# Two chained DiT blocks on one core: when the attention of block 1 waits for its PSUM banks, takes its row minima and runs its exponentials

## What is computed

```
def layer(x, cx, ...):                      # block 1, twice; the second time without context outputs
    hx = rmsnorm(x, norm_w) * (1 + scale) + shift
    px = split_cols(hx @ w_in)              # projections of the 512 latent tokens
    pc = split_cols(hc @ w_in)              # and of the 256 context tokens
    ya, yca = global_gqa(...)               # mixer A: 8 heads, keys = 512 latents + 256 context tokens
    yb, ycb = neighbourhood_attn(...)       # mixer B: 8 heads, per query block 256 context + 256 band keys
    yc_, ycc = window_gqa(...)              # mixer C: 8 heads, +-128 window + 256 context + a sink
    x = x + gate * (concat(ya, yb, yc_) * silu(px[9]) @ w_out)

# mixer A, per block of 128 queries:
    q = rmsnorm(q, qn) ; k = rmsnorm(k, kn)         # then rope
    s = einsum('bqhgd,bkhd->bhgqk', q, k_all)       # 128 x 768 scores per head
    p = softmax_f32(s)
    y = einsum('bhgqk,bkhd->bqhgd', p, v_all)
```

## Time and profile before

| | |
|---|---|
| median of 3 runs | 2501.29 us (2499.45 to 2502.21) |
| the profiled execution's own time | 2503.11 us |
| its span, first to last instruction | 2501.0 us |
| PE busy | 2406.2 us, 96% of the span |
| DVE, ACT, POOL busy | 54%, 38%, 19% |
| chain that ended last, share by engine | PE 81%, DVE 5%, ACT 5%, issue 4%, POOL 2% |
| granted PE clock, mean | 0.992 |

### The profile page before, as it was taken

How to read it: one execution, slowest core, us unless ns; L and a number is a source line. 1 busy time by engine, 2 the same in 40 slices (tenths; PEclk the granted TensorE clock), 3 DMA queues, 4 the chain that set the end, 5 groups by cost and what they waited for, 6 DMA issues and landing times.

```text
span 2501.0 us, 40281 instructions
## 1 busy us (share of the span) xinstructions
PE 2406.2 (96%) x16214; PEld 1969.1 (79%) x16214; DVE 1346.8 (54%) x2733; ACT 948.8 (38%) x1659; POOL 470.0 (19%) x287
## 2 busy tenths in 40 slices
PE   8989999999999899999999999999999999999998
PEld 6767878878877678788887668888888667888887
DVE  5667757665326654677739545333336844533333
ACT  5364263542333633554444334222225323422222
POOL 2101211012342012112474231000003241000001
PEclk9999999999999999999999999999999999999999
DMA  7302412134134044124432112223222112223222
GB/s 312 110 2 93 172 62 98 52 128 161 59 109 152 2 149 146 57 110 161 154 140 85 51 54 90 96 82 117 87 92 96 68 51 76 85 83 111 101 78 74
DMA packets 64650, 250.49 MB, mean 100 GB/s; under 512 B 7889, under 2 KB 10449, under 8 KB 54993
## 3 DMA queue, kind: packets, MB, share of 16 engines
q1 hardware_dynamic: 61216, 236.10, 26.6%
q0 software_dynamic: 2592, 11.54, 1.4%
q10 hardware_dynamic: 656, 0.30, 0.0%
HBM read 243.67 MB, written 4.19 MB: 99 GB/s over the span
## 4 chain that ended last, share of the span: by engine, by line
PE 81%; DVE 5%; ACT 5%; issue 4%; POOL 2%; DVEq 2%; DMA 1%; ACTq 1%; SPq 0%; POOLq 0%
PE ps L2650 38%; PE ps L2461 21%; PE ps L593 5%; PE ps L2627 4%; ACT probs L863 2%; PE ps L692 2%; PE ps L634 2%; DVE row_min L769 1%; PE ps L2440 1%; DVEq L772 1%; PE ps L2343 1%; PE ps L677 1%; POOL split_panels_first L1115 1%; DVE ps L780 1%; PE ps L2482 1%
## 5 line engine op out<-in xcount | busy, mean ns | idle before, releaser
L2650 PE MATMUL ps<-h_split,split_panels 128*128 128x512 f32 x2928 | 685.7, 393 | 1.8 <-ACT projected L1574 0.8
L2650 PEld LDWEIGHTS ps<-h_split,split_panels 128*128 128x128 f32 x2928 | 545.9, 188 | 126.9 <-issue 13.7
L2461 PE MATMUL ps<-h_split_first,split_panels_first 128*128 128x512 f32 (+1 forms) x2772 | 546.5, 354 | 4.1 <-POOL h_split_first L1147 2.0
L2461 PEld LDWEIGHTS ps<-h_split_first,split_panels_first 128*128 128x128 f32 x2772 | 446.1, 190 | 78.6 <-issue 8.7
L1115 POOL TENSOR_TENSOR split_panels_first<-panels_first,split_panels_first 128x1024 fp32r<-128x1024 f32 (+1 forms) x102 | 228.2, 2238 | 740.0 <-ACT split_panels_first L1302 740.0
L1984 DVE TENSOR_TENSOR split_panels<-panels,split_panels 128x1024 fp32r<-128x1024 f32 (+2 forms) x171 | 192.6, 1126 | 297.2 <-ACT split_panels L1310 293.4
L1310 ACT ACTIVATE split_panels<-panels 128x1024 fp32r<-128x1024 f32 (+2 forms) x210 | 204.3, 974 | 344.9 <-PE ps L2650 343.6
L1808 DVE SCALAR_TENSOR_TENSOR ps<-modulation_panels,silu_c,ps 128x256 f32<-128x256 f32 x480 | 225.2, 487 | 30.4 <-issue 2.1
L2650 PE MATMUL ps<-ffn_hidden_split,split_panels 128*128 128x512 f32 x990 | 225.0, 389 | 0.0
L2650 PEld LDWEIGHTS ps<-ffn_hidden_split,split_panels 128*128 128x128 f32 x990 | 185.8, 188 | 38.6
L1126 POOL TENSOR_TENSOR probs_turned<-probs_turned,probs 128x512 f32<-128x512 f32 x30 | 42.2, 1408 | 771.3 <-ACT probs L1517 771.3
(11 more groups left out here) (303 smaller groups left out, 2931.0 us busy)
## 6 DMA issues: line engine op xcount, KB each, us to landing
modulation_panels<-in_ada SPq DMA_DIRECT2D x64, 1024.0 KB, 4.8
panels<-in_w SPq DMA_DIRECT2D x88, 512.0 KB, 3.2
panels_first<-in_in SPq DMA_DIRECT2D x72, 512.0 KB, 5.7
panels<-in_in SPq DMA_DIRECT2D x42, 512.0 KB, 3.2
panels_first<-in_out SPq DMA_DIRECT2D x32, 384.0 KB, 3.0
panels<-in_w SPq DMA_DIRECT2D x32, 384.0 KB, 3.1
panels<-in_w SPq DMA_DIRECT2D x32, 320.0 KB, 2.8
panels<-in_out SPq DMA_DIRECT2D x16, 512.0 KB, 3.2
```

What stands on the lines that cost most here:

```text
L2461: ins = mm(at0, split1[:, s, w, c, :], hs1[:, h, c, lo:e], start=c == 0 and i == 0, stop=c == KC - 1 and i == 2)
L2650: ins = mm(out, split[:, n % SPLIT, a, c - base, :], moving(b, c), start=first and i == 0 and j == 0, stop=last and i == len(chunks) - 1 a ...
```

## The change

It has three parts, all in block 1's attention.

1. `scores_pe` waits at its head only for ACT's copy (the first two banks). Where the unit two before has a second copy, PE waits for DVE's copy just ahead of the first matmul that writes the third bank. Mixer A's keys also become one segment of 768 columns instead of 512 and 256, so that head 1's part in the third bank is one matmul of 512 columns instead of two of 256.
2. In mixer A (units with a `"root"`, the context units among them) one reduction takes both heads' minima, through a view of PSUM with the heads as its middle dimension, and one `scalar_tensor_tensor` multiplies both by the negated roots. `max_ready` rises by two at once.
3. In mixer B (sets of two banks) ACT runs `exponentials_act(u)` ahead of `turned_act(prev)`.

```
                     if mixer == "A":
-                        segs = [(0, 0, SEQ), (SEQ, SEQ, TOK)]
+                        segs = [(0, 0, TOK)]
...
             if u["banks_of"] and u["in_sets"]:
-                for ev in u["banks_of"]["events"][-2:]:
-                    if ev["by"] == "act":
-                        pe.wait_ge(pt_by_act, ev["c"] + 1)
-                    else:
-                        pe.wait_ge(pt_by_dve, ev["c"] + 1)
+                pe.wait_ge(pt_by_act, u["banks_of"]["events"][0]["c"] + 1)
...
             last = {}
+            third = u["banks_of"]["events"][1:] if u["banks_of"] and u["in_sets"] else []
             for e, col, a, z in segments(u):
+                if third and e == 1 and col >= 256:
+
+                    pe.wait_ge(pt_by_dve, third.pop()["c"] + 1)
...
+            if "root" in u:
+
+                s, n = 2 * u["i"] % 4, u["at"][1] - u["at"][0]
+                both_heads = ps[:, u["at"][0]:u["at"][0] + 2 * n].rearrange("p (e n) -> p e n", e=2)[:, :, 0:u["w"][0]]
+                V.tensor_reduce(row_min[:, s:s + 2], both_heads, AX_X, ALU.min)
+                dve.drain()
+                V.scalar_tensor_tensor(out=row_min[:, s:s + 2], in0=row_min[:, s:s + 2], scalar=-1.0,
+                                       in1=q_roots[:, u["root"]:u["root"] + 2], op0=ALU.mult, op1=ALU.mult).then_inc(max_ready, 2)
+                return
             for e in range(2):
...
-                    ins = V.tensor_reduce(row_min[:, s:s + 1], S, AX_X, ALU.min)
-                    if "root" in u:
-
-                        dve.drain()
-                        ins = V.scalar_tensor_tensor(out=row_min[:, s:s + 1], in0=row_min[:, s:s + 1], scalar=-1.0,
-                                                     in1=q_roots[:, u["root"] + e:u["root"] + e + 1], op0=ALU.mult, op1=ALU.mult)
-                    ins.then_inc(max_ready, 1)
+                    V.tensor_reduce(row_min[:, s:s + 1], S, AX_X, ALU.min).then_inc(max_ready, 1)
...
                 u, prev = step["unit"], step["prev"]
-                if prev:
+                copies_last = u and len(u["set"]) == 2
+                if prev and not copies_last:
                     turned_act(act, prev, o)
                 if u and not (early and u["i"] == 0):
                     exponentials_act(act, u, o)
+                if prev and copies_last:
+                    turned_act(act, prev, o)
```

## The result

The changed kernel takes 2470.53 us (median of 4 runs, 2470.0 to 2472.41) against 2500.91 (4 runs) before: a ratio of 0.9878, 95% interval 0.9866 to 0.989, or 30.4 us less. The forecast was 2475.8, 25.5 us less, in a range of 2467 to 2486.

The account below looks back on a forecast made before the run. PE was taken as held up by DVE's copy in mixer A and ACT's exponentials in mixer B; 19.7 + 5.8 = 25.5 us off 2503.1 is 2477.6, median 1.8 lower: 2475.8 us, range 2467 to 2486 (8 in 10).

Parts of the forecast that it names:

- The loop of mixer A: Mixer A: PE's scores, DVE's two reductions and copy, then PE again; a step of 5.03 us with 0.71 us of waiting.
- One reduction: Mixer A: one reduction of 1536 elements takes 1.76 us, against 2.06 us for two; exponentials and DVE's copy come 0.30 us earlier.
- (a): Mixer A: reduction at its upper bound and new hand-overs show; about 16 us gained, 2485 us; chance 0.09.
- (e): Mixer A: strided reduction runs at a fraction of the rate; about 2497 us at half, 2515 at a third; chance 0.02 slower, 0.01 even.
- The new step: Mixer A: a step falls from 5.03 to 4.31 us, bound by the exponentials, PE alone allowing 4.24; 19.7 us in all.
- The third bank's wait: Mixer A: DVE's copy is seen 0.42 us into the next scores, needed about 0.5 us in; hidden, with little to spare.
- (b): Mixer A, products to scores: the tiling mode switch drains PE, 25 by 0.3 = 7.5 us less; 18 gained, 2483 us; chance 0.04.
- The third unit and the end of a layer: Mixer A, each layer: third unit's scores about 1.0 us earlier, 0.8 kept; 0.3 kept at the last full unit.
- (c): More than forecast: all 23.5 and 7.6 us of waits go and PE's clock does not fall; 33 us, 2468 us; chance 0.07.
- 7.6 − 1.0 − 0.8 = 5.8 us: Mixer B: PE's listed waits for exponentials, less 1.0 kept by the two first stalls and 0.8 for late minima.
- The late copies in mixer B: Mixer B: ACT's copy ends about 1.5 us later, hidden; without cover it would cost 0.3 us in a few of 40 units.
- (d): Whole kernel: no change, the time is given back at the next phase; 2500 us; chance 0.05.

Follow-up runs that it names:

- part 2 alone: The kernel before with only mixer A's single reduction for both heads, scores still waiting at their head for both copies: 2491.39 us, ratio 0.9956.
- part 1 alone: The kernel before with only the wait for DVE's copy moved to the third bank and mixer A's keys in one segment: 2483.4 us, ratio 0.9921.
- the kernel with the later copy: The changed kernel with a reduction of 256 elements between the minima and DVE's copy in mixer A: 2470.56 us (one run).
- the kernel with short minima: The changed kernel with mixer A's minima taken over 640 of the 768 keys: 2467.75 us (one run).
- part 3 alone: The kernel before with only mixer B's exponentials put ahead of ACT's copies: 2490.09 us, ratio 0.995.
- the kernel with the much later copy: The changed kernel with reductions of 512 and 256 elements between the minima and DVE's copy in mixer A: 2484.05 us (one run).

## Why the forecast was right, and where it was off

**The loop of mixer A.** Read as PE, DVE, PE with the copy at its end: shown by part 2 alone, where 0.30 us less of DVE's work gave 0.30 us a step, and by part 1 alone, where the waits vanish and the step falls to the next bound.

**One reduction.** 1.76 us was forecast from the line through 256 and 768 elements, 1.758 measured. The view over two strips of PSUM has no price of its own. Rivals (a) and (e) fall with it; (a)'s step of about 4.5 is what part 1 alone gives, where the reductions are as long as (a) took them.

**The new step.** Forecast 4.31 (transposes at T+6.09, then 2.53 us to the scores after next), measured 4.333 (T+6.07, then 2.60). The transposes last 0.99 us for 24 here instead of 0.93, and that is most of the 0.07. That the exponentials bind, and PE only just behind, is shown from both sides: 4.273 when the minima come sooner, 4.50 when they come later. The forecast also had small new waits of the transposes on ACT in mixer A. They are there, but only in the row of the weight loads. Mixer A of layer 2, before (805 to 890 us) and then in the changed kernel (785 to 860 us); in the rows of the matmuls neither has such a wait:

```profile
PEld ps L634 <- ACT probs L863: 0.4, 1, 0.4
```

```profile
PEld ps L634 <- ACT probs L866: 3.8, 14, 0.5
```

**The third bank's wait.** Forecast as hidden with little to spare: the copy would end 0.27 us into the scores and be seen 0.42 us into them. It is hidden, but the room is larger than I gave it: in the kernel with the later copy it ends 0.58 us and is seen 0.63 us into the scores, and that costs nothing.

**The mode switch.** In the changed kernel the products end, as modelled, at 134.41 + 1.48 = 135.89, and the scores in the other tiling start at 135.82, 0.07 us sooner, as in mixer B's row. The 4.273 us of the kernel with short minima leave about 0.03 us a step beyond the 4.24 that the rows gave, where rival (b) wanted 0.3. So (b) falls. The Trainium skill ("TensorEngine Tiling (Array Packing)", Key Properties) says that a change of tiling mode drains TensorE; no run here shows whether it does, only that it costs no more than this.

**The third unit and the end of a layer.** The third unit's wait fell from 2.24 to 1.1 us (forecast about 1.2). Layer 1 came out at 10.2, as forecast, but two small misses cancel in it: the twelve steps behind the fourth unit gave 8.6 us (forecast 8.4), and from the last full unit on 0.07 us was left instead of 0.3, since one step of the context units takes 2.51 us instead of 2.27.

Layer 2 gave 11.3 instead of 9.5. Its twelve steps gave 8.65 (forecast 8.4) and its end 0.3, as forecast. The rest is the third and the fourth unit: the fourth starts 2.3 us sooner after the second, where the forecast had 0.8. In layer 1 the same two units gave 1.5, the forecast's 0.8 and one step of 0.7. In layer 2 the forecast missed that step: it counted listed waits, and the fourth unit (824.91 us before) had none. The last 0.8 us is a slow stretch that went: before, the step from the third to the fourth unit took 5.76 us in layer 2 and 4.99 in layer 1. There PE's granted clock was 0.72 before, at 1.2 GHz for a part of the stretch. In the changed kernel's windows it is 1.00, 2.4 GHz, from the first scores of that mixer to the last:

```profile
788.00:860.00 72.00, 69.61 (x906) 52.87 (x905) 48.46 (x91) 48.37 (x80) 2.35 (x1) 1.00 0.01 4
```

So 0.8 us of rival (c) came true. Whether the shorter stall kept the clock up can be read from all eleven kernels, though none was made for it. At the third unit of layer 2 the three that stall for 1.8 us or more (the kernel before, part 2 alone, part 3 alone) all show a clock of 0.72 in the 6 us behind, and the eight that stall for 1.13 us show 1.00. In layer 1 it is less clear: the same 2.24 us left the clock at 1.00 in the kernel before, and it fell to 0.73 in part 3 alone; and behind a stall of 1.13 us it fell to 0.72 in the kernel with the much later copy. The stall goes with the fall, but does not decide it alone.

**Mixer B, the term that was mis-sized.** The step that failed is "7.6 − 1.0 − 0.8 = 5.8 us": 9.0 measured, above my bound of 7.6. I took the listed waits of PE as all that could be gained. They are not. The kernel before, two steps of mixer B:

```profile
363.20 1.14 PE L593 MATMUL ps<-qkv 64*128 64x256 f32 x8
364.36 0.71 PE L634 MATMUL ps<-matrices,probs 64*128 64x64 f32 x16
...
366.83 1.13 PE L593 MATMUL ps<-qkv 64*128 64x256 f32 x8
367.80 0.66 PE L634 MATMUL ps<-matrices,probs 64*128 64x64 f32 x16
```

The same two in the changed kernel:

```profile
346.89 1.13 PE L593 MATMUL ps<-qkv 64*128 64x256 f32 x8
347.86 0.66 PE L634 MATMUL ps<-matrices,probs 64*128 64x64 f32 x16
...
350.28 1.13 PE L593 MATMUL ps<-qkv 64*128 64x256 f32 x8
```

At 364.36 no wait is listed, as the transposes start just 0.02 us behind the modelled end of the scores. But where nothing holds them they start 0.97 us after the scores (366.83 to 367.80), 0.16 ahead of that end; here it is 1.16, and they take 0.71 instead of 0.66 us. So 0.24 us was lost with no idle time to show for it, and the step went from 3.63 to 3.39 us (346.89 to 350.28). The same 0.2 us belongs on top of the listed waits: 5.0 us in layer 1 and 14 times 0.2 are 7.8, less some 2 us that are left on the same count, and 5.6 were gained. The weight loads' row, which the forecast did not use, had it. Waits of PE's weight loads from 318 to 440 us, before:

```profile
PEld ps L634 <- ACT probs L863: 11.4, 16, 1.8
```

and at the same place in the changed kernel (304 to 425 us):

```profile
PEld ps L634 <- ACT probs L866: 3.4, 6, 0.9
```

8.0 us less, where the row of the matmuls would have had 5.0 at most, and 5.6 were gained. The truth lies between the two rows, since a weight load's wait is in part beside running matmuls. My correction for stalls that come from late minima was right: the three of 0.25 us in layer 1 are still there. And the first stall of each layer fell from 1.4 to 0.5, as forecast. PE's waits in mixer B of the changed kernel, layer 1 (304 to 425 us) and then layer 2 (950 to 1020 us):

```profile
PE ps L634 <- ACT probs L866: 1.2, 4, 0.5
```

```profile
PE ps L634 <- ACT probs L866: 0.5, 1, 0.5
```

**The late copies in mixer B.** No wait of line 692 on ACT's copies is among PE's waits in mixer B of the changed kernel, so the price was nothing, as forecast.

**No change, given back later (d).** The phases between and behind are as long as before but for 1.1 us in all; the time carried through.

## What to carry to other kernels

When a wait covers several signals, ask which part of the work behind it needs which one, and price the move by the next loop, not by the wait: here 0.71 us of stall gave 0.69, because a second edit moved the next bound (the exponentials) by just enough, and alone it gave 0.5. A loop that runs over two steps shows half of what you add to it or take from it. Read the waits of the weight loads beside those of the matmuls: a stall shorter than the overlap of modelled ends leaves no idle time in the matmul rows. And whether a consumer may run ahead of a copy depends on how many sets of buffers there are: with three (mixer B) the exchange gave 9 us, with two (mixer C) it cost 83.

## What the runs showed that I had not expected

A wait in the middle of a block of matmuls can be free: the weight load for the third bank waited 0.33 us in the kernel with the later copy, and the block stayed at 1.89 us. And the granted clock can fall behind added stalls: with 71 us of new waits in mixer C it had a mean of 0.84 over 115 us.
